# Hybrid decoder trunk on one core: the order of VectorE's softmax work in a head's step, and of the loads, tables and first products of the opening

## The chip, the cores and the metric

One core of a Trainium2 chip runs the whole program. The time is device time of that core in microseconds (us), from launch to end. The engines are TensorE (PE, its weight loads PEld), VectorE (DVE), ScalarE (ACT), GpSimd (POOL) and SyncE (SP, which issues most DMAs). Each has its own instruction stream, in the order in which the program is written; they meet at semaphores.

## What is computed

Two post-norm decoder layers over 256 tokens of 1024 features, float32. The part that matters here, cut from the reference:

```python
def hybrid_mixer(x, positions, w_in, ...):
    h = x @ w_in
    c_q, c_kv, k_rope, fox_qkv, fox_f, dil_qkv = jnp.split(h, cuts, axis=-1)
    q_a = to_heads(rms_norm(c_q, q_gain) @ w_uq, MLA_HEADS)        # 4 heads "MLA"
    kv_a = to_heads(rms_norm(c_kv, kv_gain) @ w_ukv, MLA_HEADS)
    ...
    o_b = causal_block_attention(q_b, k_b, v_b, cum_log_f)          # 6 heads "FOX"
    o_c = dilated_mixture_attention(rope(q_c, positions), rope(k_c, positions), v_c)   # 6 heads "DIL"
    return mixed @ w_out

for l in range(2):
    x = layer_norm(ALPHA * x + hybrid_mixer(x, ...), ...)
    x = layer_norm(ALPHA * x + memory_cross_attention(x, mem, ...), ...)
    gates = shared_group_router(x, router_w, router_bias)            # top-1 group, top-2 experts
    x = layer_norm(ALPHA * x + moe_ffn(x, gates, ...), ...)
```

Every softmax is over the keys of one query; a dilated head's exponentials are multiplied by how often a key falls into the three windows, and then summed.

## The kernel before

**Weights.** All weights come as a stream of pieces of up to 128x1024 float32, in the order of `weight_stream`: per layer A (4 pieces: the latents), FV, FK, FQ, UQ, UKV, DQ, DK, DV, MK, MV0, WO0, WO1 and so on, then the experts. SP loads a piece into a ring of 12 places (`raw`); a load waits until the piece 12 before it has been split. ACT copies a piece to its high part (`split_hi`, L562), DVE subtracts to get the low part (`split_lo`, L568); the two parts stand in a ring of 4 places (`w_split`), and a place is free when PE has used the piece (`split_free`). PE takes three products for each chunk, high*high, high*low, low*high (`product`, L1646 to L1648).

**The opening of layer 0.** x comes as two tiles of 128 tokens (XT0, XT1). PE turns each (`turn_x`, 8 transposes, L1737), ACT takes the high part (L759) and DVE the low part (L1119) into xT. PE then works through A (`gemm`, `rows`: each piece for token tile 0 and 1 in turn, banks 0 and 1), turns the memory tokens (`turn_memory`, L1635), and goes on with FV and FK. `warm(n)` (L1772) is n transposes of the identity whose result nobody reads. `constants` and `make_angles` are small DVE tables. POOL loads gains, forget bias and router bias with `small(0)` and one more DMA (L588 to L597), from its own queue (q0); SP's loads run in queue q1.

**Heads.** A loop over 20 steps `s` runs on PE, DVE and ACT; in a step each engine works on another of the 16 heads. PE's step: the products of the pieces `turns[l][s]` (one to three, mostly one), the values of heads s-5 and s-4 at odd s (`head_values`, L1865), the transposes of head s-3's probabilities (`head_turn`, L1844), the scores of head s-1 (`head_scores`, L1819 and L1820; for the DIL heads both of a pair at odd s, L1810), and the transposes of head s's q and k (`head_qk`). `head_turn` waits for the scaled probabilities of its head and for the copy of the head before it, since all use one PSUM bank (B_PT). DVE's step is in this order:

```python
                    for h in scored(s):
                        softmax_max(l, h)
                    if TURNED <= s < HEADS + TURNED:
                        evac_pT(l, s - TURNED)
                    if 2 <= s < HEADS + 2:
                        softmax_norm(l, s - 2)
                    for i in ahead_of[l][s]:
                        split_lo(dve, i)
                    if s >= VALUED and (s - VALUED) % 2 == 1:
                        ...
                        evac_o(l, s - VALUED)
```

`softmax_max` (L1142, L1145) writes scaled, masked scores to SBUF with their maximum, and then its negative; `softmax_norm` (L1161 for DIL heads, L1164, L1168) sums, inverts and scales the exponentials; `evac_pT` (L1178) copies transposed probabilities out of PSUM; `evac_o` (L1188) makes the low part of the heads' outputs (`mixT_lo`). ACT makes the exponentials (`exps`, L804) one step before `softmax_norm` takes them. `ahead_of[l][s]` are the pieces that PE uses two steps later. `rotate` (L658 to L664) is the rotary work on POOL.

**Before the experts.** The router's group choice `ing` (L1314) is DVE work; `gather` on PE waits for it. In layer 0 products of layer 1's memory keys stand ahead of that wait; in layer 1 `keep_busy(11)` does (L1767: 11 products of 128x512 that nobody reads).

## Time and profile before

| | us |
|---|---|
| median of 3 runs | 809.81 (809.38 to 812.72) |
| the profiled execution, its own time | 808.45 |
| span of its trace, first to last instruction | 806.8 |
| busy in it: PE / DVE / ACT / POOL | 785.0 / 629.0 / 506.8 / 77.4 |

The profiled execution is 1.36 us under the median of the three runs; 1.65 us of its time lie outside the span. Matmuls are pipelined and their ends are modelled, so a row of PE tells when it starts; how long a wait is, is best read from start to start. Engine rows that follow without a gap are merged with "x n".

### The profile page before, as it was taken

The page shows a single profiled execution, that of the slowest core. Times are in us where ns is not written, and L with a number is a line of the kernel's source. Part 1 is how long each engine was busy: PE and PEld are TensorE (multiplying, and loading weights), DVE is VectorE, ACT ScalarE, POOL GpSimd, SP SyncE. Part 2 cuts the span into 40 slices and gives each one's busy share as a digit, 9 for nine tenths or more (in the row PEclk, how much of TensorE's full clock was granted, in tenths as well). Part 3 has the DMA queues.
Part 4 walks back from the last instruction along what each step waited for, and adds up shares of the span by engine and source line. Part 5 has one row for each costly group of instructions (what it writes and reads, how often), then busy time and mean ns, then how long its engine had stood idle before and what let it go on. Part 6 is the DMA issues. An engine that isn't in the chain of part 4 may idle for free.

```text
span 806.8 us, 12012 instructions
## 1 busy us (share of the span) xinstructions
PE 785.0 (97%) x4311; PEld 677.0 (84%) x4311; DVE 629.0 (78%) x1110; ACT 506.8 (63%) x782; POOL 77.4 (10%) x150
## 2 busy tenths in 40 slices
PE   8999999999999999999999999989999999999995
PEld 7999996789888888888899988868998788888884
DVE  5657777785669999999874578887655799999995
ACT  4755564454547788888756566544443768888873
POOL 3159000020000000000011233002000000000000
PEclk9999999999999999999999999999999999999998
DMA  9964343575345799999956543426634349999951
GB/s 294 362 203 158 132 132 106 161 226 164 105 147 166 232 365 371 365 365 372 350 150 181 170 131 131 148 99 200 211 105 131 131 148 347 370 365 366 370 198 53
DMA packets 123117, 177.05 MB, mean 219 GB/s; under 512 B 10176, under 2 KB 92624, under 8 KB 123056
## 3 DMA queue, kind: packets, MB, share of 16 engines
q1 hardware_dynamic: 121072, 169.56, 62.9%
q0 software_dynamic: 1984, 6.70, 3.0%
q8 instruction: 36, 0.59, 0.3%
q14 instruction: 25, 0.20, 0.1%
HBM read 175.18 MB, written 1.05 MB: 218 GB/s over the span
## 4 chain that ended last, share of the span: by engine, by line
PE 86%; DVE 10%; issue 1%; DMA 1%; ACT 1%; DVEq 0%; SPq 0%; ACTq 0%
PE bank L1646 24%; PE bank L1648 23%; PE bank L1647 23%; DVE w_split L568 2%; PE bank L1831 2%; PE bank L1874 2%; PE bank L1844 2%; PE bank L1865 1%; DVE xg_lo L1582 1%; PE bank L1820 1%; PE bank L1984 1%; PE bank L1737 1%; PE bank L1800 1%; PE bank L1894 1%; DVE xs L1194 1%
## 5 line engine op out<-in xcount | busy, mean ns | idle before, releaser
L568 DVE TENSOR_TENSOR w_split<-raw,w_split 128x1024 fp32r<-128x1024 f32 (+3 forms) x334 | 383.7, 1172 | 68.6 <-ACT w_split L562 63.3
L562 ACT ACTIVATE w_split<-raw 128x1024 fp32r<-128x1024 f32 (+3 forms) x334 | 334.4, 1010 | 107.6 <-PE bank L1648 92.5
L1646 PE MATMUL bank<-w_split,xg_hi 128*128 128x512 f32 x256 | 102.9, 402 | 0.0
L1648 PE MATMUL bank<-w_split,xg_lo 128*128 128x512 f32 x256 | 100.1, 391 | 0.0
L1647 PE MATMUL bank<-w_split,xg_hi 128*128 128x512 f32 x256 | 99.9, 390 | 0.0
L1646 PE MATMUL bank<-w_split,xT_hi 128*128 128x384 f32 (+2 forms) x224 | 77.8, 347 | 0.1
L1648 PE MATMUL bank<-w_split,xT_lo 128*128 128x384 f32 (+2 forms) x224 | 75.8, 338 | 0.0
L1647 PE MATMUL bank<-w_split,xT_hi 128*128 128x384 f32 (+2 forms) x224 | 75.6, 338 | 0.0
L1648 PEld LDWEIGHTS bank<-w_split,xg_lo 128*128 128x128 f32 x256 | 48.0, 188 | 10.3
L1646 PEld LDWEIGHTS bank<-w_split,xg_hi 128*128 128x128 f32 x256 | 48.1, 188 | 9.4 <-DVE xg_lo L1582 0.5
L1647 PEld LDWEIGHTS bank<-w_split,xg_hi 128*128 128x128 f32 x256 | 48.2, 188 | 9.0
L1646 PE MATMUL bank<-w_split,mixT_hi 128*128 128x512 f32 x128 | 51.8, 404 | 2.0 <-DVE w_split L568 1.9
L1648 PE MATMUL bank<-w_split,mixT_lo 128*128 128x512 f32 x128 | 50.0, 391 | 0.0
L1647 PE MATMUL bank<-w_split,mixT_hi 128*128 128x512 f32 x128 | 50.0, 390 | 0.0
L1648 PE MATMUL bank<-w_split,aT_lo 128*128 128x512 f32 x128 | 49.8, 389 | 0.0
L1646 PE MATMUL bank<-w_split,aT_hi 128*128 128x512 f32 x128 | 49.8, 389 | 0.0
L1647 PE MATMUL bank<-w_split,aT_hi 128*128 128x512 f32 x128 | 49.8, 389 | 0.0
L1646 PEld LDWEIGHTS bank<-w_split,xT_hi 128*128 128x128 f32 x224 | 42.2, 188 | 1.1 <-DVE w_split L568 0.6
L790 ACT ACTIVATE qkT<-bank 66x512 f32<-66x512 f32 (+2 forms) x26 | 15.5, 595 | 42.9 <-PE bank L1800 29.5
L1647 PEld LDWEIGHTS bank<-w_split,xT_hi 128*128 128x128 f32 x224 | 42.3, 189 | 0.1
L1648 PEld LDWEIGHTS bank<-w_split,xT_lo 128*128 128x128 f32 x224 | 42.1, 188 | 0.0
L1178 DVE COPY probs<-bank 128x384 f32<-128x384 f32 (+1 forms) x40 | 23.3, 582 | 19.1 <-PE bank L1848 12.1
(325 smaller groups left out, 1531.4 us busy)
## 6 DMA issues: line engine op xcount, KB each, us to landing
raw<-in_expert_w_gate_dram SPq DMA_DIRECT2D x128, 256.0 KB, 5.9
raw<-in_expert_w_up_dram SPq DMA_DIRECT2D x128, 256.0 KB, 7.7
raw<-in_expert_w_down_dram SPq DMA_DIRECT2D x64, 512.0 KB, 7.7
raw<-in_xattn_w_kv_dram SPq DMA_DIRECT2D x32, 512.0 KB, 3.8
raw<-in_w_in_dram SPq DMA_DIRECT2D x40, 384.0 KB, 4.5
raw<-in_w_mix_out_dram SPq DMA_DIRECT2D x16, 512.0 KB, 3.4
raw<-in_xattn_w_q_dram SPq DMA_DIRECT2D x16, 512.0 KB, 3.4
raw<-in_xattn_w_o_dram SPq DMA_DIRECT2D x16, 512.0 KB, 5.3
```

Of the source, the lines that this page charges most:

```text
L562: nc.scalar.activation(halves_of(i)[0][:, 0:w], raw[:, i % RAW, 0:w], ACT.Copy).then_inc(hi_ready, 1)
L568: nc.vector.tensor_tensor(lo[:, 0:w], raw[:, i % RAW, 0:w], hi[:, 0:w].bitcast(F32), ALU.subtract).then_inc(lo_ready, 1)
L790: nc.scalar.activation(qkT[0:d, qk_slot(h), :], B_QK[0:d, :], ACT.Copy).then_inc(qkT_ready.sem, n)
L1178: nc.vector.tensor_copy(turned_of(h), B_PT[:, 0:w]).then_inc(pT_ready.sem, 1)
L1194: nc.vector.scalar_tensor_tensor(half, half, ALPHA, product, ALU.mult, ALU.add, accum_out=st[:, 2 * n_ + t, 2 * h:2 * h + 1]).then_inc(sig ...
L1582: nc.vector.tensor_tensor(xg_lo[:, f, :, :].rearrange("p g s -> p (g s)"), bank[XG_BANKS[f]][:, :], xg_hi[:, f, :, :].rearrange("p g s -> ...
L1646: nc.tensor.matmul(o, lhs[0], rhs[0], start=first, stop=False, skip_group_check=shared)
L1647: nc.tensor.matmul(o, lhs[0], rhs[1], start=False, stop=False, skip_group_check=shared)
L1648: return nc.tensor.matmul(o, lhs[1], rhs[0], start=False, stop=last, skip_group_check=shared)
L1831: ins = nc.tensor.matmul(o[:, t * T:(t + 1) * T], qTx[:, 2 * g + c_, t * P:(t + 1) * P], kTx[:, 2 * g + c_, :], start=c_ == 0, stop=c_ == 1)
L1844: ins = nc.tensor.transpose(B_PT[:, k * P:(k + 1) * P], pr[:, k * P:(k + 1) * P], ident[:, :])
L1874: ins = nc.tensor.matmul(value_bank(h)[:, dblk * T:(dblk + 1) * T], vx[:, c_, f * P:(f + 1) * P], turned_of(h)[:, c_ * T:(c_ + 1) * T], st ...
```

## The change

Four parts.

1. **DVE's step.** `softmax_norm(s-2)` moves to the front of the step, ahead of `softmax_max` and `evac_pT`. `softmax_max` of the 16 heads multiplies by minus the scale and takes the minimum, so that it writes the negated maximum itself, and its own negation (L1145) falls away; ACT's `exps` use scale -1, and wait for each token tile by itself. For the 6 DIL heads `evac_pT` moves to ACT, behind `evac_o` and ahead of the copies and `evac_qk`.
2. **The opening's products.** `warm(8)` is removed. XT0 and XT1 use banks 4 to 7 instead of 0 to 3. A's first three pieces are done for token tile 0 first and then for tile 1 (`by_tile`). ACT's and DVE's split of A's second piece stands ahead of XT1.
3. **The opening's loads and tables.** SP issues positions and memory tokens behind FV's four pieces instead of behind A's. POOL's four small loads wait until FV's second piece has landed, and stand behind its masks. DVE's and ACT's work on memory (`turn_memory`), angles and sines, and the A latents stand in another order; PE waits for the memory's low parts before UQ instead of before FK.
4. **Ahead of `gather` in layer 1** `keep_busy(11)` becomes `keep_busy(7)`.

The diff, cut:

```diff
@@ -304,6 +304,8 @@
...
         def pair_in(l, name, k):
+            if l == 0 and name in ("XT0", "XT1"):
+                return k + 2
             return 1 - k if l and k < 2 and job[name] >= job["MV0"] else k
@@ -534,7 +536,7 @@
...
                     tokens(1)
-                if i == index[0, "A", 3]:
+                if i == index[0, "FV", 3]:
                     sp.dma_start(pos_i[:, :], positions[0].rearrange("(t p) -> p t", p=P),
                                  allow_slow_non_contiguous=True).then_inc(pos_in, 16)
@@ -683,6 +683,10 @@
...
+            pool.wait_ge(raw_in[index[0, "FV", 1] % RAW], landed_value[index[0, "FV", 1]])
+            pool.nop().then_inc(paused_p, 1)
+            small(0)
+            pool.dma_start(rbias[:, :], router_bias.rearrange("(a n) -> a n", a=1).to_broadcast([P, NE])).then_inc(bias_in, 16)
             pool.wait_ge(mem_in, 16)
@@ -789,14 +793,21 @@
...
+            def evac_pT(l, h):
+                act.wait_ge(pt_done.sem, pt_done.at(l, h + 1))
+                act.wait_ge(o_done.sem, o_done.at(l, h - 1))
+                nc.scalar.activation(turned_of(h), B_PT[:, 0:3 * P], ACT.Copy).then_inc(pT_ready.sem, 1)
+
             def exps(l, h):
-                act.wait_ge(nmx_ready.sem, nmx_ready.at(l, h + 1))
+                if h >= HEADS:
+                    act.wait_ge(nmx_ready.sem, nmx_ready.at(l, h - HEADS + 1))
                 if h >= 3:
                     act.wait_ge(pt_done.sem, pt_done.at(l, free_turns(h)))
                 for t in range(TT):
                     if h < HEADS:
+                        act.wait_ge(s_masked.sem, s_masked.at(l, 2 * h + t + 1))
                         sl = slice(0, P) if t == 0 else slice(P, 3 * P)
-                        src, scale = probs_of(h)[:, sl], 1.0
+                        src, scale = probs_of(h)[:, sl], -1.0
@@ -882,14 +893,12 @@
                 turn_x(l, "XT0", 0)
                 if l:
                     turn_later(l)
+                    split_hi(act, first + 1)
                 else:
+                    split_hi(act, first + 1)
                     turn_x(l, "XT1", 1)
-                split_hi(act, first + 1)
                 for i in range(first + 2, first + 8):
                     split_hi(act, i)
-                if l == 0:
-                    turn_memory()
-                    sines()
@@ -927,6 +942,8 @@
                 for s in range(HEADS + VALUED):
                     if s >= VALUED and (s - VALUED) % 2 == 1:
                         evac_o(l, s - VALUED)
+                    if MLA_H + FOX_H + TURNED <= s < HEADS + TURNED:
+                        evac_pT(l, s - TURNED)
@@ -1139,10 +1155,8 @@
                     scale = float(MLA_D if h < MLA_H else HD) ** -0.5
                     for t in range(TT):
                         sl = slice(0, P) if t == 0 else slice(P, 3 * P)
-                        nc.vector.tensor_tensor_reduce(probs_of(h)[:, sl], score_bank(h)[:, sl], mask[:, P - P * t:2 * P], scale, -3e38,
-                                                       ALU.add, ALU.max, mx[:, h, t:t + 1]).then_inc(s_masked.sem, 1)
-                    dve.wait_ge(s_masked.sem, s_masked.at(l, 2 * h + 2))
-                    nc.vector.tensor_scalar(nmx[:, h, :], mx[:, h, :], -1.0, None, ALU.mult).then_inc(nmx_ready.sem, 1)
+                        nc.vector.tensor_tensor_reduce(probs_of(h)[:, sl], score_bank(h)[:, sl], mask[:, P - P * t:2 * P], -scale, 3e38,
+                                                       ALU.add, ALU.min, nmx[:, h, t:t + 1]).then_inc(s_masked.sem, 1)
@@ -1430,22 +1446,25 @@
...
+                    split_lo(dve, first + 1)
+                else:
                     split_lo(dve, first)
-                split_lo(dve, first + 1)
+                    turn_x(l, "XT0", 0)
+                    split_lo(dve, first + 1)
+                    turn_x(l, "XT1", 1)
                 split_lo(dve, first + 2)
                 split_lo(dve, first + 3)
                 if l == 0:
                     constants()
+                split_lo(dve, first + 4)
+                if l == 0:
                     make_angles()
-                for i in range(first + 4, first + 8):
+                for i in range(first + 5, first + 8):
                     split_lo(dve, i)
-                if l == 0:
-                    turn_memory()
@@ -1453,8 +1472,14 @@
...
-                for i in range(first + 8, first + 12):
-                    split_lo(dve, i)
+                split_lo(dve, first + 8)
+                split_lo(dve, first + 9)
+                if l == 0:
+                    turn_memory(range(2))
+                split_lo(dve, first + 10)
+                if l == 0:
+                    turn_memory(range(2, 4))
+                split_lo(dve, first + 11)
@@ -1494,12 +1519,12 @@
...
+                    if 2 <= s < HEADS + 2:
+                        softmax_norm(l, s - 2)
                     for h in scored(s):
                         softmax_max(l, h)
-                    if TURNED <= s < HEADS + TURNED:
+                    if TURNED <= s < MLA_H + FOX_H + TURNED:
                         evac_pT(l, s - TURNED)
-                    if 2 <= s < HEADS + 2:
-                        softmax_norm(l, s - 2)
                     for i in ahead_of[l][s]:
                         split_lo(dve, i)
@@ -1665,6 +1690,25 @@
...
+            def by_tile(l, js):
+
+                open_job(l, "A")
+                parts = {}
+                for t, b in enumerate(banks(l, "A")):
+                    last_half = evac_v[l][job[f"XT{t}"]]
+                    pe.wait_ge(job_v.sem, job_v.at(l, last_half - 1))
+                    for j in js:
+                        if t == 0:
+                            parts[j] = sub_in(index[l, "A", j])
+                        if j == 2:
+                            pe.wait_ge(job_v.sem, job_v.at(l, last_half))
+                        for k in range(2):
+                            lhs = tuple(v[:, 2 * j + k, t * P:(t + 1) * P] for v in xT)
+                            r = tuple(v[:, k * A_W:(k + 1) * A_W] for v in parts[j])
+                            ins = product(b[:, 0:A_W], lhs, r, j == 0 and k == 0, False)
+                        if t == TT - 1:
+                            ins.then_inc(split_free, 1)
@@ -1923,7 +1967,7 @@
...
                 else:
-                    keep_busy(11)
+                    keep_busy(7)
@@ -2049,21 +2093,22 @@
...
                     turn_x(l, "XT1", 1, 0)
-                    warm(8)
-                ready(l, "XT0")
-                pe.wait_ge(job_v.sem, job_v.at(l, evac_v[l][job["XT1"]] - 1))
-                for i in range(first + 0, first + 2):
-                    gemm(i)
-                ready(l, "XT1")
-                for i in range(first + 2, first + 4):
-                    gemm(i)
+                if l:
+                    ready(l, "XT0")
+                    pe.wait_ge(job_v.sem, job_v.at(l, evac_v[l][job["XT1"]] - 1))
+                    for i in range(first + 0, first + 2):
+                        gemm(i)
+                    ready(l, "XT1")
+                    gemm(first + 2)
+                else:
+                    by_tile(l, range(3))
+                gemm(first + 3)
                 if l == 0:
                     turn_memory()
                 for i in range(first + 4, first + 8):
                     gemm(i)
                 if l == 0:
                     pe.wait_ge(fp_tables, 3)
-                    pe.wait_ge(mem_v, 4)
```

What the change does to the order, at three places. First PE's opening of layer 0, before (bank7 with ident alone is `warm`):

```order
1 L1772 MATMUL bank7<-ident_57 128x128 x12
2 L1737 MATMUL bank0<-ident_57,xs_51 128x128 x4
4 L1737 MATMUL bank2<-ident_57,xs_51 128x128 x4
6 L1772 MATMUL bank7<-ident_57 128x128 x8
7 L1646 MATMUL bank0<-w_split_50,xT_hi_52 128x416
10 L1646 MATMUL bank1<-w_split_50,xT_hi_52 128x416
```

and the same place in the changed kernel:

```order
1 L1816 MATMUL bank7<-ident_57 128x128 x12
2 L1781 MATMUL bank4<-ident_57,xs_51 128x128 x4
4 L1781 MATMUL bank6<-ident_57,xs_51 128x128 x4
6 L1671 MATMUL bank0<-w_split_50,xT_hi_52 128x416
24 L1671 MATMUL bank1<-w_split_50,xT_hi_52 128x416
```

Eight transposes are gone, and 18 products of tile 0 (bank 0) now stand ahead of tile 1's first (bank 1), which were three.

Second, DVE at step 15 of layer 0, where the scores of heads 14 and 15 are taken, from the second of the two maxima, before (L1142 is `softmax_max`, L1178 `evac_pT`, L1161 to L1168 `softmax_norm` of head 13):

```order
206 L1142 ISA probs,mx<-bank,dilmask 128x256
207 L1142 ISA mx 128x1
208 L1145 TENSOR_SCALAR nmx<-mx 128x2
209 L1178 COPY probs<-bank 128x384
210 L1161 ISA probs,sm<-probs,dilcount 128x128
214 L1164 RECIPROCAL ri<-sm 128x2
215 L1168 TENSOR_SCALAR probs<-probs,ri 128x128
216 L1168 TENSOR_SCALAR probs<-probs,ri 128x256
217 L568 TENSOR_TENSOR w_split<-raw,w_split 128x1024
218 L1188 TENSOR_TENSOR mixT_lo<-bank,mixT_hi 128x256
```

and after, from the end of `softmax_norm` of head 13 (L1182):

```order
195 L1182 TENSOR_SCALAR probs<-probs,ri 128x256
196 L1158 ISA probs,nmx<-bank,dilmask 128x128
198 L1158 ISA probs,nmx<-bank,dilmask 128x256
200 L1158 ISA probs,nmx<-bank,dilmask 128x128
202 L1158 ISA probs,nmx<-bank,dilmask 128x256
204 L570 TENSOR_TENSOR w_split<-raw,w_split 128x1024
205 L1202 TENSOR_TENSOR mixT_lo<-bank,mixT_hi 128x256
```

The scaling has gone ahead of the maxima, the negation and the copy are gone, and the split of the next piece follows the second maximum directly.

Third, ACT in the same steps, before (L812 is `evac_o`, L804 `exps`):

```order
99 L812 ACTIVATE mixT_hi<-bank 128x256
100 L562 ACTIVATE w_split<-raw 128x1024
101 L804 ACTIVATE probs<-probs,nmx 128x128
102 L804 ACTIVATE probs<-probs,nmx 128x256
105 L562 ACTIVATE w_split<-raw 128x1024
```

and after (L799 is the copy `evac_pT`):

```order
105 L823 ACTIVATE mixT_hi<-bank 128x256
106 L799 ACTIVATE probs<-bank 128x384
107 L564 ACTIVATE w_split<-raw 128x1024
108 L815 ACTIVATE probs<-probs,nmx 128x128
112 L799 ACTIVATE probs<-bank 128x384
113 L564 ACTIVATE w_split<-raw 128x1024
```

Each step of the DIL heads has one copy more on ACT, ahead of the split.

## Rows read from the trace of the kernel before

**Rows 1.** The page: the chain that ended last, by engine.

```profile
PE 86%; DVE 10%; issue 1%; DMA 1%; ACT 1%; DVEq 0%; SPq 0%; ACTq 0%
```

**Rows 2.** PE's waits, 60 to 172 us (heads of layer 0): total, times, longest.

```profile
PE bank L1844 <- DVE probs L1168: 1.6, 2, 0.9
PE bank L1646 <- DVE w_split L568: 0.9, 2, 0.7
```

**Rows 3.** PE's waits, 457 to 565 us (heads of layer 1).

```profile
PE bank L1844 <- DVE probs L1168: 2.2, 3, 0.9
PE bank L1646 <- DVE w_split L568: 1.0, 2, 0.7
```

**Rows 4.** PE, 530 to 543 us: start, duration, work, [idle before it].

```profile
530.97 0.39 PE L1648 MATMUL bank<-w_split,mixT_lo 128*128 128x512 f32 x1
532.23 0.55 PE L1844 MATMUL bank<-ident,probs 128*128 128x128 f32 x3 [0.87 <-DVE probs L1168]
533.45 0.47 PE L1646 MATMUL bank<-w_split,mixT_hi 128*128 128x512 f32 x1 [0.68 <-DVE w_split L568]
...
541.47 0.87 PE L1865 MATMUL bank<-probs,dv 128*64 128x256 f32 x8 [0.65 <-DVE probs L1178]
```

**Rows 5.** DVE in order of time, 530 to 533 us.

```profile
530.27 0.56 DVE L1178 COPY probs<-bank 128x384 f32<-128x384 f32 x1
...
532.08 1.22 DVE L568 TENSOR_TENSOR w_split<-raw,w_split 128x1024 fp32r<-128x1024 f32 x1
```

**Rows 6.** DVE in order of time, 468 to 474 us.

```profile
468.50 0.55 DVE L1168 TENSOR_SCALAR probs<-probs,ri 128x128 f32<-128x128 f32 x2
...
471.07 0.29 DVE L1142 CUSTOM_DVE_ANT_0 probs<-bank,causal 128x128 f32<-128x128 f32 x1 [0.91 <-PE bank L1820]
...
472.49 1.50 DVE L1168 TENSOR_SCALAR probs<-probs,ri 128x128 f32<-128x128 f32 x2
```

**Rows 7.** PE in order of time, 9 to 21 us.

```profile
9.61 1.91 PE L1772 MATMUL bank<-ident 128*128 128x128 f32 x8
11.38 0.58 PE L1646 MATMUL bank<-w_split,xT_hi 128*128 128x416 f32 x1
...
11.99 0.35 PE L1648 MATMUL bank<-w_split,xT_lo 128*128 128x416 f32 x1
12.18 0.35 PE L1646 MATMUL bank<-w_split,xT_hi 128*128 128x416 f32 x1
...
20.64 1.91 PE L1635 MATMUL bank<-ident,mem_tok 128*128 128x128 f32 x16
```

**Rows 8.** ACT, then DVE, in order of time, 7 to 20 us.

```profile
18.40 0.86 ACT L562 ACTIVATE w_split<-raw 128x780 fp32r<-128x780 f32 x1 [0.20 <-DMA raw<-in_w_in_dram]
19.45 0.86 ACT L562 ACTIVATE w_split<-raw 128x780 fp32r<-128x780 f32 x1 [0.20 <-DMA raw<-in_w_in_dram]
...
7.66 1.28 DVE L1119 TENSOR_TENSOR xT_lo<-bank,xT_hi 128x512 fp32r<-128x512 f32 x2
10.48 1.29 DVE L1119 TENSOR_TENSOR xT_lo<-bank,xT_hi 128x512 fp32r<-128x512 f32 x2 [1.54 <-ACT xT_hi L759]
```

**Rows 9.** Queue q0, 6 to 11 us; A's second piece; POOL's wait for memory.

```profile
q0 software_dynamic: 143, 0.21, 40.6%
...
L503 SPq DMA_DIRECT2D raw<-in_w_in_dram x1: 433/433/433, 2.3 to 2.3; - x1
...
DMA to landing us min/median/max: 8.3/8.3/8.3
...
16.85 0.56 POOL L672 DMA_DIRECT2D gb<-in_ln_mix_g_dram  x1 [9.72 <-DMA mem_tok<-in_mem_dram]
```

**Rows 10.** Layer 1 ahead of gather: PE, DVE, and busy time with granted clock.

```profile
639.29 4.36 PE L1767 MATMUL bank<-memT_hi,ones 128*128 128x512 f32 x11
...
642.36 0.17 DVE L1314 TENSOR_TENSOR ing<-rt 128x8 fp32r<-128x8 f32 x1
...
640.00:642.00 2.00, 2.00 (x6) 1.54 (x5) 1.73 (x11) 1.97 (x3) 0.00 (x0) 0.50 0.66 254
```

30 lines of the change are left out of this document (18 added, 12 removed).

## The prediction

> **What bounds the kernel now.** I read the chain that ended last first: PE has 86% of it and DVE 10% [rows 1]. So the end moves only where PE waits, or where it does work that nobody needs. There are three such places. PE's waits in the heads of layer 0 are 1.6 us for scaled probabilities and 0.9 us for a split [rows 2]; in layer 1 they are 2.2 and 1.0 us [rows 3], and one of 0.65 us for a copy [rows 4]. Next the opening: from 9.61 us PE does eight dummy transposes, and A's products begin at 11.38 us [rows 7]. Last, ahead of gather in layer 1, eleven dummy products begin at 639.29 us and take about 4.2 us, though `ing`, for which PE waits behind them, is made at 642.36 us (0.17 us long) [rows 10].
>
> In order of time the waits in the heads show what is late. PE starts the last product of a piece at 530.97, and the transposes of head 13 only at 532.23: 1.26 us where these products follow each other every 0.23 us, so 1.03 us are lost, of which the row calls 0.87 idle [rows 4]. DVE was meanwhile at the copy of 530.27, then at head 13's scaling, and turned to the split of the next piece at 532.08, which takes 1.22 us; that split ends at 533.3, and PE's next piece starts at 533.45 [rows 4, 5]. The exponentials of head 13 are a step old by then: the scaling is late only because it stands behind work that waits for PE's newest scores.
>
> **The heads.** The added order costs nothing by itself: same instructions, less one negation (about 0.17 us, by the small DVE instruction of L1314 [rows 10]) in each of 32 steps. With the scaling first, `head_turn` need not wait: in layer 1 head 13's scaling starts as soon as DVE is free, before the scores. Behind the scores DVE then has two maxima and, with the copy gone to ACT, goes directly to the split. At 530.27 the maxima were over; without two negations they end near 530.1, but the scaling of about 1.3 us, now ahead of them, partly pushes them to about 530.5. The split then ends near 531.7 instead of 533.3, and PE gains 1.0 us on the transposes and 0.65 us on the next piece, 1.65 us here. The same pair of waits stands in layer 0. Idle times of 2.5 us in layer 0 and 3.85 us in layer 1 are 6.3 us over ten waits [rows 2 to 4]; from start to start the example loses 0.16 us more (1.03 against 0.87) [rows 4]; on some eight of them that is 1.3 us, so at most 7.6 us. What stays: the wait at 541.47, head 15's values, is 0.65 us, and it is the way from transposes to copy to values; ACT's copy of such a tile is hardly shorter than DVE's 0.56 us, so I leave 0.5 us of it [rows 4, 5]. That gives **7.1 us**. The lower bound is nothing, if each wait goes over to another releaser; the upper 7.6.
>
> What hides the moved work: DVE idles 0.91 us before a maximum [rows 6], and a clean scaling is 0.55 us for its two tiles [rows 6]. Beside POOL's rotary work the same two instructions took 1.50 us [rows 6]; there the front of the step overflows by about 0.8 us (0.15 of reciprocal with it), and maximum, exponentials and copy come that much later. PE asks for that copy only behind the next piece's 12 products, 2.1 us at least (an estimate for 128x384, from 0.19 us for 128x416 [rows 7]), so I cost it at nothing; without this cover it would be 0.8 us in some four steps a layer. The six copies on ACT stand ahead of `evac_qk` and the splits; ACT is busy for 506.8 of 806.8 us and has them at the same PE event for which it waits in that step anyway, so nothing.
>
> At this place a rule of the Trainium skill bears. SBUF — State Buffer, section "SBUF: two separate sides", says that DVE in a two-port mode and GpSimd share one port pair as an exclusive lock, held for a whole instruction. The trace agrees (0.55 against 1.50 us [rows 6]). By it, what matters is under which POOL work the scaling falls, not how long it is; it speaks against putting it ahead of the maxima, and by it the sum would be some 6 us smaller at worst (0.8 us, four steps, two layers), which I take up as a rival from the rows.
>
> **The opening.** Without the eight transposes A's first products could start at 9.61 [rows 7]. They need tile 0's low part, from 7.66 on two instructions of 1.28 us together, so 8.9 [rows 8]; in the order of before they would also need tile 1's first half, half of the 1.29 us from 10.48, so 11.1 [rows 8]: `by_tile` is what makes the 1.8 us usable. But the eight dummies started every 0.22 us (1.77 us from 9.61 to 11.38), half the pace of the sixteen of the memory, which take 1.91 us; the products of 128x416 follow every 0.19 us from 11.99 on [rows 7]. So until about 11.7 PE is at the lower of its two clock levels (1.2 against 2.4 GHz), and the first six products take about 2.1 us instead of 1.1. After them comes A's second piece: it landed at 10.6 (2.3 + 8.3) [rows 9], while POOL's small loads held 40.6% of the DMA engines from 6 to 11 us, 2.0 us of them [rows 9]. With these loads later I take 8.6, and its low part at 10.5: no wait. The third piece lands near 10.5, is split behind tile 1 on both engines, and is there at 12.9, some 0.05 to 0.1 us late. Then 42 more products at 0.19 us: A ends near 19.65 instead of 20.64 [rows 7]. **1.0 us.** Bounds: if the second piece still lands at 10.6, everything behind it is 1.9 us later, and A ends about 0.9 us later than before; at best (no slow clock) it ends 1.8 us earlier.
>
> The memory tokens come next. They had landed by 16.85 [rows 9]; behind FV's four pieces they land where FV's fourth did. Its second was taken at 18.40 and its third at 19.45, both just as they landed, so one piece is 1.05 us of queue and the fourth landed at 20.5, the latest that I allow [rows 8]; but as the small loads' 2.0 us are issued only after FV's second piece has landed, most of them fall behind the memory: 18 to 18.5. PE asks at 19.65: no wait, and 0.85 us at the upper bound. The rest of part 3 (latents, angles, sines, memory parts) I cost at nothing: PE reads none of it before FK's end, 18 us later.
>
> The Trainium skill, TensorE: Matmul & The Clock Gate, section "Part 4: PE-mode transpose", says that transposes do not count as PE-busy for the clock. By the trace the products kept the full pace 0.6 us after the first had started, behind 36 transposes and nothing else (28 of them before 9.61) [rows 7], so here they count. By the page the eight dummies did nothing, and their removal would leave the products alone to raise the clock: about 1 us more of slow products, and the opening would gain nothing.
>
> **Gather.** The granted clock from 640 to 642 us was 0.50 [rows 10], so each dummy took about 0.4 us. Seven end near 641.9, `ing` is there at 642.5, and PE goes on at 642.5 instead of 643.5: 1.0 us in an execution with this low clock. At full clock eleven take about 2.5 us and end before `ing`: nothing. And if the idle 0.6 us keep the clock low, PE's eight products of 128x512 behind it take 1.8 us longer. I take **0.5 us** (bounds -0.8 and 1.0).
>
> **Sum.** 7.1 + 1.0 + 0.5 = 8.6 us. Against the profiled execution (808.45) that is 799.85; it was 1.36 us under the median of the runs, and the median is the measure: 809.81 - 8.6 = **801.2 us**. Behind these places PE's chain has no clock of its own to wait for, so I expect nothing to be given back.
>
> **The rivals.**
> - *The waits change their releaser.* Behind the turned wait stands the split (0.68 of its own at 533.45) and the low part of the outputs; one that stays late keeps half of the heads' gain: 7.1 to 3.5, 804.8 us. For it: DVE's next work is already behind. Against: it was late only by the scaling and the copy. Chance 0.15.
> - *The opening gives nothing*: the second piece lands late, or the clock stays low as the page's rule would have it, or PE waits for memory; 1.0 becomes 0 to -0.9, so 802.2 to 803.1 us. Chance 0.12.
> - *Slower than before.* The scaling at the front waits for ACT's exponentials of the step before, and holds the maximum behind it. Place: every step of both layers; price: what exponentials end later than the scores, plus the scaling (0.7 us clean, 1.65 beside POOL) less DVE's 0.91 us of idle. It decides against the change from 0.27 us lost on PE in each of 32 head steps, 8.6 us; at 0.4 us the time is 814. Against: exponentials were done before the scores in the steps of which rows show waits, and PE has a piece of 2.1 us between. With the POOL steps alone, up to 6 us are lost, 807. Chance 0.07 (0.04 of it above 813).
> - *More than I count*: shorter steps also take away small delays before the transposes of q and k; 798. Chance 0.06.
>
> My forecast, 799 to 803.5 us, has 0.60. The range 798.5 to 805.5 leaves out the slow rival and the ends of the first and the last. A measurement tells about 0.5%, 4 us, from no change. Faster by over that (under 805.8): 0.60 + 0.12 + 0.06 + 0.08 of the first rival = 0.86; within: 0.10; slower: 0.04.
>
> **What would show it.** Right: no wait of the head transposes (L1844 before) on the scaling in either layer; 1 us or less of PE waits left in each; A's first product near 9.6, with five slow ones behind it; memory transposes near 19.7; POOL's small loads at 13 to 16 us. Wrong: `softmax_norm` preceded by long idle on ACT's exponentials, or by PE waits on qkT or the maxima; A's second piece split after 11 us; PE waiting for mem_tok; a granted clock of 0.5 behind gather or in the opening past 12 us.

## The result, and where the time went

The changed kernel takes **803.91 us** in the median of four runs (803.51 to 804.43), against 809.92 us (809.38 to 812.72) of the kernel before in the same session: ratio 0.9915, 95% interval 0.9891 to 0.9938, so it is between 5.0 and 8.8 us faster. Forecast were 801.2 us and a saving of 8.6; the measured time lies 0.4 us above the 799 to 803.5 us that were held most likely, and inside the range of 798.5 to 805.5. The profiled execution took 803.51 us with a span of 801.9 us, where that of before had 806.8. In the chain that ended last PE's share has grown from 86% to 88%, and DVE's has fallen from 10% to 8% [rows 1]:

```profile
PE 88%; DVE 8%; issue 1%; ACT 1%; DMA 1%; DVEq 0%; SPq 0%; ACTq 0%
```

PE's waits, by what it waited for (us in total, times, longest): from 60 to 172 us there is none left [rows 2]. From 457 to 565 us, in the heads of layer 1 [rows 3], all waits for scaled probabilities are gone, and of the others one, for a split, has grown to 1.4 us:

```profile
PE bank L1671 <- DVE w_split L570: 1.4, 1, 1.4
PE bank L1909 <- ACT probs L799: 0.6, 1, 0.6
```

The surest reading of such a pair of traces is to take the PE instruction at the same place in the order in both and to subtract its starts. The difference is the time saved up to there; it is flat over hundreds of instructions and steps only where something happened. Inside A, where the order of the products differs, it compares equal counts of products: the 13th is the first of A's second piece before, and the first of its third piece after.

| PE instruction | start before | start after | saved |
|---|---|---|---|
| A's 13th product | 13.88 | 13.06 | 0.82 |
| first transpose of the memory tokens (end of A) | 20.64 | 19.91 | 0.73 |
| transposes behind the first wait of layer 0's heads | 74.11 | 72.47 | 1.64 |
| first output piece behind layer 0's heads | 144.53 | 140.46 | 4.07 |
| a product of layer 1's memory keys, behind layer 0's router | 250.65 | 247.66 | 2.99 |
| piece behind head 13's transposes, layer 1 | 533.45 | 526.14 | 7.31 |
| piece behind head 15's values, layer 1 | 542.69 | 536.40 | 6.29 |
| first dummy product ahead of gather, layer 1 | 639.29 | 634.90 | 4.39 |
| first product for `ing` | 643.49 | 638.19 | 5.30 |
| last product of PE | 797.04 | 791.87 | 5.17 |

So the opening gave 0.7 to 0.8 us, and the heads by these rows 3.25 and 4.3 us less 1.0. Counted over the heads alone (from the starts of 59.98 and 457.00 us of before) they gave 3.3 and 4.5 us less 1.0, 6.7 in all; the rest is small differences between the two. Ahead of the `ing` products there are two places at which time was **lost** that was already saved: 1.1 us in layer 0 and 1.9 us in layer 1. Both stand under half clock. Busy time in stretches of 2 us (PE, PEld, DVE, ACT, POOL, granted clock, DMA share, GB/s) of the changed kernel, layer 0 and then layer 1:

```profile
242.00:244.00 2.00, 2.00 (x21) 2.00 (x20) 1.74 (x3) 1.13 (x2) 0.49 (x1) 1.00 0.47 193
244.00:246.00 2.00, 2.00 (x16) 2.00 (x16) 1.73 (x9) 1.82 (x3) 0.00 (x0) 0.80 1.05 272
246.00:248.00 2.00, 2.00 (x11) 2.00 (x11) 1.07 (x8) 0.84 (x2) 0.00 (x0) 0.50 0.86 281
...
628.00:630.00 2.00, 0.76 (x5) 0.53 (x6) 1.74 (x4) 1.69 (x4) 0.00 (x0) 1.00 0.04 15
630.00:632.00 2.00, 2.00 (x15) 2.00 (x15) 1.79 (x3) 1.94 (x3) 1.04 (x2) 0.72 0.10 18
632.00:634.00 2.00, 2.00 (x11) 2.00 (x11) 1.23 (x1) 0.12 (x1) 0.00 (x0) 0.50 0.99 356
634.00:636.00 2.00, 2.00 (x8) 1.81 (x9) 0.59 (x3) 0.91 (x2) 0.00 (x0) 0.50 0.95 293
```

In the trace of the kernel before, the only half clock between the opening and the end began at 639.77 us, under the dummies [rows 10]. There it cost at most what the dummies ran past the making of `ing`, about 1 us. Now it begins at 630.89 us, under the router's products, on which everything waits. The rows of PE show the same by pace: the first router group takes 0.60 us for four products, those behind it 1.0 us. Gather's products follow right behind the seven dummies:

```profile
630.30 0.60 PE L2211 MATMUL bank<-w_split,xT_hi 128*128 128x32 f32 x4
630.75 0.89 PE L2216 MATMUL bank<-w_split,xT_lo 128*128 128x16 f32 x4
631.49 1.01 PE L2211 MATMUL bank<-w_split,xT_hi 128*128 128x32 f32 x4
...
634.90 3.15 PE L1811 MATMUL bank<-memT_hi,ones 128*128 128x512 f32 x7
638.19 0.27 PE L1974 MATMUL bank<-ing,upto 128*128 128x4 f32 x1
```

The new wait at the end of layer 1's heads is read from ACT and DVE, in order of time. ACT stands idle for 2.61 us until PE's transposes of head 15 are done, copies them, and only then makes the two splits that are queued behind; DVE's half of the first split, for which PE waits 1.43 us, starts at 535.03:

```profile
530.46 0.49 ACT L799 ACTIVATE probs<-bank 128x384 f32<-128x384 f32 x1
533.57 0.49 ACT L799 ACTIVATE probs<-bank 128x384 f32<-128x384 f32 x1 [2.61 <-PE bank L1888]
533.95 1.99 ACT L564 ACTIVATE w_split<-raw 128x1024 fp32r<-128x1024 f32 x2
```

```profile
536.40 0.47 PE L1671 MATMUL bank<-w_split,mixT_hi 128*128 128x512 f32 x1 [1.43 <-DVE w_split L570]
```

Before, the copy was DVE's, and ACT made the same two splits directly behind the head outputs.

The opening, PE in order of time. The eight transposes of tile 1 take 1.09 us, and the products behind them run at 0.19 us from the start, so PE was at its upper clock level; the granted clock reads full from 6.25 us on. In place of slow products there are two waits, for the low parts of A's second and third piece:

```profile
7.88 1.09 PE L1781 MATMUL bank<-ident,xs 128*128 128x128 f32 x8 [1.32 <-DMA xs<-in_x_dram]
8.73 0.43 PE L1671 MATMUL bank<-w_split,xT_hi 128*128 128x416 f32 x1
9.00 0.35 PE L1672 MATMUL bank<-w_split,xT_hi 128*128 128x416 f32 x1
...
10.93 0.46 PE L1671 MATMUL bank<-w_split,xT_hi 128*128 128x416 f32 x1 [0.82 <-DVE w_split L570]
...
13.06 0.46 PE L1671 MATMUL bank<-w_split,xT_hi 128*128 128x416 f32 x1 [0.73 <-DVE w_split L570]
...
19.91 1.25 PE L1660 MATMUL bank<-ident,mem_tok 128*128 128x128 f32 x10
```

### The profile page after: what moved, and what is told of

It reads as the page before. It is cut to its first block, busy times and chain, and to the rows that moved or that the text cites. A ratio compares the mean times of both kernels' runs of the same rounds, so it can differ in the third digit from the quotient of the medians.

```text
span 801.9 us, 11957 instructions
## 1 busy us (share of the span) xinstructions
PE 782.4 (98%) x4299; PEld 677.3 (84%) x4299; DVE 620.0 (77%) x1066; ACT 511.7 (64%) x794; POOL 79.3 (10%) x150
## 4 chain that ended last, share of the span: by engine, by line
PE 88%; DVE 8%; issue 1%; ACT 1%; DMA 1%; DVEq 0%; SPq 0%; ACTq 0%
PE bank L1671 24%; PE bank L1673 24%; PE bank L1672 24%; DVE w_split L570 2%; PE bank L1875 2%; PE bank L1918 2%; PE bank L1888 2%; PE bank L1909 1%; DVE xg_lo L1607 1%; PE bank L1844 1%; PE bank L1864 1%; PE bank L1938 1%; DVE xs L1208 1%; DMA raw<-in_w_in_dram 1%; PE bank L1781 1%
## 5 line engine op out<-in xcount | busy, mean ns | idle before, releaser
L1671 PE MATMUL bank<-xT_hi,w_split 128*128 128x256 f32 x112 | 32.4, 289 | 0.0
```

The costliest lines, as they stand in the source:

```text
L1671: nc.tensor.matmul(o, lhs[0], rhs[0], start=first, stop=False, skip_group_check=shared)
```

## The experiments

Twelve further runs were made, one of them the changed kernel again. The theory for all: each part removes what the start-to-start table shows, independently of the others, and the rest of the difference to the forecast is half clock. The rivals: the parts shift waits to each other; or ACT's copies, not the place of the scaling, make the heads' gain. "Saved" is always by PE's starts against the kernel before; for the heads it is counted over the heads alone, as above.

### The heads alone, and the opening alone

Heads alone is the kernel before with only `softmax_norm`, `softmax_max`, `exps` and `evac_pT` of the diff; opening alone is the rest of it, with eleven dummies.

> The kernel before with the heads' part alone (scaling at the front, negated scores, six copies on ACT). In the trace of the changed kernel PE's starts in the heads of layer 0 come 3.25 us earlier than before, in layer 1 4.32 us earlier and then 1.03 us of it are lost again. If the parts are independent, this kernel gains the sum, 6.5 us of 809.9: 803.4 us, with no PE wait over 0.3 us in the heads of layer 0, and with waits of about 0.6 and 1.4 us at the end of the heads of layer 1. Stretches of half clock may move the time by 1 to 3 us either way, and the saving from start to start between them should stay 6.5. Rival (the opening shifts DVE's and POOL's work under the heads and gives part of it): under 5 us from start to start.

> The kernel before with the opening's parts alone (no dummies, products by tile, loads and tables moved; 11 dummies ahead of gather, heads as before). A ends 0.8 us earlier, nothing else moves: 809.1 us, PE's waits in the heads 2.5 and 3.9 us as before. In the changed kernel's trace the clock was full from 6.25 us on, before only from 11.71; if the full clock again comes at 6.25 the waits for the second and third piece (0.8 us each) stand, and if it comes late the first products are slow instead and A ends about as much earlier (0.5 to 0.9 us). Rival (the whole 0.8 us was the earlier clock): with full clock from 11 us on nothing is saved at the end of A.

Heads alone: 803.86 us (803.05 to 805.87), ratio 0.9918 (0.9895 to 0.9941). The heads save 3.3 us in layer 0 and 4.5 less 1.0 in layer 1, the same steps as in the whole change, at the same instructions: 6.7 us. The rival, that the opening feeds the heads' gain, falls. Opening alone: 809.0 us, ratio 0.9979 (0.9961 to 0.9996): 1.7 us faster, with 0.3 to 3.2 inside the interval.

The opening of before, in the trace of the heads' run, showed a wait of PE that had not been there:

```profile
19.47 1.91 PE L1642 MATMUL bank<-ident,mem_tok 128*128 128x128 f32 x16
32.05 0.41 PE L1653 MATMUL bank<-w_split,xT_hi 128*128 128x384 f32 x1 [2.12 <-DVE w_split L568]
```

In that execution PE was 1.2 us ahead of [rows 7] at the memory transposes, without any change of the opening: the granted clock rose at 5.42 us instead of 11.71. It lost this and more at FK. DVE makes FK's low parts behind the latents (29.65 us; 28.49 before), which wait for ACT's squares, and these stood behind memory copies and a table load. About half of the wait has another source: FV's fourth piece landed later in this execution, and ACT took it at 22.04 us instead of 20.90, behind 1.45 us of waiting for it:

```profile
22.04 0.85 ACT L562 ACTIVATE w_split<-raw 128x780 fp32r<-128x780 f32 x1 [1.45 <-DMA raw<-in_w_in_dram]
```

None of the twelve traces with the new order has a wait at FK: the latents come at 24.3 to 27.4 us there. So the order of latents, memory and sines, which I had priced at nothing, seems to be what lets PE keep a gain made further ahead. No run moves this order by itself, so its own share is not shown.

The opening alone also showed what its two new waits can bring, by the granted clock:

```profile
12.00:14.00 2.00, 1.27 (x5) 1.23 (x5) 2.00 (x5) 0.04 (x1) 0.58 (x1) 0.71 1.08 387
14.00:16.00 2.00, 2.00 (x8) 1.92 (x7) 0.38 (x4) 0.00 (x0) 1.76 (x4) 0.50 1.04 383
```

The saving stood at 1.14 us at A's 13th product and at -0.55 behind this stretch: 1.7 us lost.

### The small loads back at their old place

```diff
+            small(0)
+            pool.dma_start(rbias[:, :], router_bias.rearrange("(a n) -> a n", a=1).to_broadcast([P, NE])).then_inc(bias_in, 16)
             nc.gpsimd.memset(causal[:, :], 0.0).then_inc(const_pool, 1)
...
             pool.wait_ge(raw_in[index[0, "FV", 1] % RAW], landed_value[index[0, "FV", 1]])
             pool.nop().then_inc(paused_p, 1)
-            small(0)
-            pool.dma_start(rbias[:, :], router_bias.rearrange("(a n) -> a n", a=1).to_broadcast([P, NE])).then_inc(bias_in, 16)
```

> The changed kernel with POOL's small loads and the router's bias at their old place, at POOL's start. If they delay A's second piece: its low part is ready at 12 to 12.5 us instead of 10.88, PE's wait ahead of the second piece is 2 us or more instead of 0.85, and A ends 1 us or more later, after the kernel before: 804.9 us. Rival (the second piece is bound by ACT and DVE, which split it): PE's wait stays at 0.8 us, and A ends at the same time.

805.65 us (804.08 to 808.01), ratio 0.9937 (0.9898 to 0.9976). ACT in order of time: the second piece is taken 2.56 us later than in the changed kernel (8.91):

```profile
11.47 0.90 ACT L564 ACTIVATE w_split<-raw 128x832 fp32r<-128x832 f32 x1 [3.60 <-DMA raw<-in_w_in_dram]
```

The saving at A's 13th product is -1.74 us instead of +0.82. So the opening's gain hangs on the moved loads; with the products by tile and without the dummies, but with the loads at their old place, the opening ends 1.8 us later than before. The expected low part at 12 to 12.5 us started at 12.40; PE's wait ahead of it is 1.15 us, less than the 2 expected, since here the clock rose late and the first products were slow.

### The heads' two halves: copies back on DVE, scaling back at the end

```diff
-                    if MLA_H + FOX_H + TURNED <= s < HEADS + TURNED:
-                        evac_pT(l, s - TURNED)
...
-                    if TURNED <= s < MLA_H + FOX_H + TURNED:
+                    if TURNED <= s < HEADS + TURNED:
                         evac_pT(l, s - TURNED)
```

> The changed kernel with the six copies of transposed probabilities back on DVE, between the maxima and the split; the scaling stays at the front and the scores negated. If the scaling's place alone removes PE's waits for scaled probabilities and the copies those for the split: from start to start the heads of layer 0 save 1.9 us instead of 3.25 (0.8 and 1.0 at the transposes, nothing at the splits) and those of layer 1 2.7 us instead of 4.3, but the loss of 1.03 us at their end is gone, since no copy stands before ACT's splits: 4.6 instead of 6.55 in all, some 805.5 us. Rival (the scaling does it all, DVE had slack for the copy): 3.25 and 4.3 with no loss at the end, 7.5 in all, 802.8 us.

```diff
-                    if 2 <= s < HEADS + 2:
-                        softmax_norm(l, s - 2)
                     for h in scored(s):
                         softmax_max(l, h)
                     if TURNED <= s < MLA_H + FOX_H + TURNED:
                         evac_pT(l, s - TURNED)
+                    if 2 <= s < HEADS + 2:
+                        softmax_norm(l, s - 2)
```

> The changed kernel with the scaling of DVE's step back at its old place behind the maxima (and behind the copies of the other heads); negated scores and ACT's copies stay. DVE then has 0.17 us of negation and 0.55 us of copy less ahead of the scaling, so of each wait of about 1 us for scaled probabilities 0.7 us go: if it is so, the heads of layer 0 save 2.5 to 3 us and those of layer 1 3.5 to 4, and the place of the scaling was worth 1 us or less. Rival (the place is what counts): the five waits for scaled probabilities stand at 0.5 us or more each and the heads save under 4 us together.

Copies on DVE: 803.09 us (802.54 to 805.06), ratio 0.9923 (0.9906 to 0.9940), saved 2.7 us in layer 0 and 4.1 in layer 1 with nothing lost at its end, 6.8 together, as much as with ACT's copies (6.7). PE's waits in its layer 1:

```profile
PE bank L1907 <- DVE probs L1190: 0.6, 1, 0.6
PE bank L1669 <- DVE w_split L570: 0.4, 1, 0.4
```

Scaling at the end: 809.76 us, ratio 0.9998 (0.9983 to 1.0013), saved 1.4 us in layer 0 and nothing in layer 1 (1.0 won, 1.0 lost at its end). PE's waits in its layer 1:

```profile
PE bank L1671 <- DVE w_split L570: 2.1, 2, 1.4
PE bank L1888 <- DVE probs L1182: 1.4, 2, 0.7
PE bank L1909 <- ACT probs L799: 0.6, 1, 0.6
```

I had expected the opposite division (most of the gain without the place of the scaling), and that fell. With ACT's copies and the negated scores in both, the place is worth 5.3 of the 6.7 us. Two of the three waits for scaled probabilities in layer 1 stayed, behind the products of 470.87 and 488.01 us, 0.97 and 1.09 us from start to start as before. They are those of heads 1 and 5, whose copies are DVE's in both kernels; the third, head 13's, whose copy is now ACT's, is gone. Nor did the missing negation help these two. At head 5 DVE comes to the scaling sooner behind its maxima, but its two instructions then take 1.78 us instead of 1.49, and they end 0.15 us behind the end of POOL's rotary instruction of 487.89 us:

```profile
486.60 0.55 DVE L1192 COPY probs<-bank 128x384 f32<-128x384 f32 x1
487.26 1.78 DVE L1182 TENSOR_SCALAR probs<-probs,ri 128x128 f32<-128x128 f32 x2
```

```profile
487.89 1.00 POOL L660 TENSOR_TENSOR rot<-dk,sinb 128x384 f32<-128x384 f32 x1
```

The negation by itself was not run: no kernel here has the scaling at the front and the scores not negated. By DVE's rows its removal shortens the maxima of one head from 0.76 to 0.56 us and those of a pair from 1.63 to 1.12; what share of the 5.3 us needs it is not shown.

### Splits ahead of the last copy

```diff
+                    held = l and s == HEADS + TURNED - 1
-                    if MLA_H + FOX_H + TURNED <= s < HEADS + TURNED:
+                    if MLA_H + FOX_H + TURNED <= s < HEADS + TURNED and not held:
                         evac_pT(l, s - TURNED)
...
                     for i in ahead_of[l][s]:
                         split_hi(act, i)
+                    if held:
+                        evac_pT(l, s - TURNED)
```

> The changed kernel with one reordering on ACT in layer 1: the two splits of the last head steps stand ahead of the copy of head 15's transposed probabilities instead of behind it. If that copy, which waits for PE's transposes, is what made the splits late (ACT idle 2.61 us before it, then the split at 533.95, DVE's half at 535.03, PE's wait of 1.43 us), the wait is gone and the end of the heads comes 1.0 to 1.4 us earlier: 802.7 us. Rival (the splits wait for their piece or their slot anyway): the same splits at the same time and no gain, and the copy late by up to 2 us, 804 to 806 us.

By the trace the theory holds. ACT makes the two splits first and does the copy behind them, and PE's wait for the split is gone, the one for the copied probabilities (0.58 us) stays:

```profile
531.82 0.49 ACT L799 ACTIVATE probs<-bank 128x384 f32<-128x384 f32 x1
532.21 2.00 ACT L564 ACTIVATE w_split<-raw 128x1024 fp32r<-128x1024 f32 x2
534.93 0.49 ACT L799 ACTIVATE probs<-bank 128x384 f32<-128x384 f32 x1 [0.71 <-PE bank L1891]
```

The saving goes from 5.95 to 6.42 us there instead of from 7.31 to 6.29: 1.5 us. The time does not show it: 805.15 us (803.28 to 806.05), ratio 0.9928 (0.9905 to 0.9952). In the profiled execution there was half clock from 12.9 to 16.3, 245.0 to 248.4 and 630.7 to 644.4 us, in which 1.6, 1.2 and 3.5 us of saved starts went again. By the time alone it would have been read as a loss.

### Dummies ahead of gather, and in the idle stretch ahead of the router

```diff
-                    keep_busy(7)
+                    keep_busy(11)
```

> The changed kernel with 11 dummy products again instead of 7 ahead of gather in layer 1. If the stretch there is at half clock: four dummies of 0.42 us more, 1.3 to 1.7 us behind the making of ing, so 804.8 to 805.5 us. If it is at full clock: eleven take 2.5 us, ing is made 3.2 us after the last score product, no difference. Rival (dummies are what brings the full clock back): with 11 the full clock returns earlier and the time is equal or under that of 7.

```diff
-                    keep_busy(6)
+                    keep_busy(12)
```

> The changed kernel with twelve dummy products instead of six in layer 1 while PE waits for the second half of the normalized tokens: PE's idle stretch of 1.41 us there is filled (six at 0.23 us). If that idle stretch is what brings the clock down behind it (half clock from 630.89 to 637.71), there is no half clock between 626 and 645, the router's products save 1.9 us, and the seven dummies ahead of gather end early and cost nothing: 2 to 3 us less than the changed kernel's 803.9, or 801.5 us. Rival (the router's narrow products of 16 and 32 columns are what it answers to, or it comes by chance of where it falls): half clock stands again somewhere between 630 and 645 and the time is that of the changed kernel.

Eleven: 802.17 us (801.86 to 804.34), ratio 0.9895 (0.9873 to 0.9916). I had expected it to be slower than the changed kernel under half clock, and it was not. Twelve ahead of the transposes, with seven behind: 803.14 us (800.73 to 803.36), ratio 0.9909 (0.9892 to 0.9925). PE is fed there and the clock holds until 633.8 us, through all the router's products, so the 1.9 us that the changed kernel lost there are kept (the repeat below, which is not fed, kept them too, so this does not show the feeding). But the clock falls under the dummies. The seven, four of them still at full clock, end early, PE idles for `ing`, and gather runs at half clock behind it:

```profile
632.81 2.49 PE L1811 MATMUL bank<-memT_hi,ones 128*128 128x512 f32 x7
636.09 0.37 PE L1974 MATMUL bank<-ing,upto 128*128 128x4 f32 x1 [0.79 <-DVE ing L1330]
```

```profile
634.00:636.00 2.00, 1.30 (x4) 0.49 (x2) 1.69 (x12) 1.97 (x4) 0.00 (x0) 0.50 0.92 258
636.00:638.00 2.00, 1.91 (x7) 1.81 (x8) 1.40 (x6) 2.00 (x3) 0.00 (x0) 0.50 0.29 102
638.00:640.00 2.00, 2.00 (x6) 1.52 (x6) 2.00 (x3) 0.52 (x1) 0.00 (x0) 0.50 0.04 8
```

Over all traces the two numbers of dummies differ by about 1 us in the mean. Saved from the end of layer 1's heads (the product that starts at 542.69 us before) to PE's end; where half clock lay within 535 to 545 us of a kernel's own time, from behind it:

| kernels with | saved, each trace | mean |
|---|---|---|
| seven dummies | -1.1, -3.5, -0.8, -1.1, -0.8, -0.7, -0.9 | -1.3 |
| eleven dummies | 0.0, 0.0, -1.6, -0.1, -0.1, +0.3 | -0.2 |

Gather ran at half clock in five of the seven traces with seven dummies; with eleven, in one of six and there for its first 0.8 us. (In the row of seven, one trace, and in the row of eleven, two have the twelve ahead of the transposes as well.) In four of these traces (both of -1.1, the -3.5 and the -1.6) half clock began under the router's products, well ahead of the dummies, so not all of the difference is gather's. Where it began within 1.2 us of the dummies' start, it lasted 3.4 us in each of the five traces with eleven and in that of before, and 6.8 us in each of the four with seven. So the early end of the seven did not bring half clock on; the half clock was there already, and stayed longer.

### The changed kernel again, and three steps on top of each other

The repeat; then splits first with eleven dummies; then with twelve ahead of the transposes as well; and then, in the opening:

```diff
                         if t == 0:
+                            if j:
+                                for _ in range(5):
+                                    nc.tensor.transpose(bank[2][:, 0:P], ident[:, :], ident[:, :])
                             parts[j] = sub_in(index[l, "A", j])
```

> The changed kernel itself again, as the bar for the other three of this call: PE's starts save 0.8 us in the opening, 3.3 in the heads of layer 0 and 3.3 in those of layer 1, as in its first trace. If the stretches of half clock are a matter of where they fall in an execution, at least one of them (245.18 to 248.59 and 630.89 to 637.71 in the first trace) begins at another place or is missing; if they follow from the order of the work, both stand at the same places within 1 us. 803.9 us either way.

> The changed kernel with the two splits ahead of the last copy in layer 1, and eleven dummies ahead of gather again. The splits save 1.5 us at the end of the heads of layer 1, as in the trace of the run that moved them alone. Seven dummies that end early leave PE idle for about 1.2 us ahead of gather and gather then ran at half clock in three traces; if the eleven avoid that, 1 to 2 us more: 801.0 us. Rival (the half clock comes with eleven as well, as in the trace of the run with eleven alone, and the dummies only cost): 803 us or the time of the repeat.

> The run with the splits moved and eleven dummies, and twelve dummies instead of six ahead of the second half's transposes in layer 1. With PE fed at both places the only stretch with little activity is that of the router's narrow products: if the idle stretches bring the half clock, there is none between 626 and 650 us and it takes 2 us less than the run with the splits and eleven dummies, 799.5 us. Rival (the narrow products are enough, as in layer 0, where no idle stands ahead of the half clock at 245 us): half clock stands there still, and it is 0 to 1 us faster.

> The run before with five dummy transposes ahead of each of PE's two waits for A's second and third piece (0.85 and 0.8 us idle in the changed kernel's trace). In two of six traces with these waits the clock fell at 12.9 us, for 1.65 us lost. If the idle brings that, the stretch is gone, and with full clock at 6 us the transposes (0.11 us each) cost nothing: 0.5 us less in the median. Rival (where the clock comes late, at 11.4 to 11.7 us, the transposes take 0.21 us each and stand in PE's way): up to 1 us slower than the run before.

| kernel | median, us | range | ratio to before |
|---|---|---|---|
| changed kernel again | 802.97 | 800.12 to 805.74 | 0.9903 (0.9877 to 0.9930) |
| splits first, eleven dummies | 801.84 | 799.56 to 802.75 | 0.9885 (0.9862 to 0.9908) |
| and twelve ahead of the transposes | 801.03 | 798.64 to 801.94 | 0.9878 (0.9855 to 0.9900) |
| and the opening fed | 800.91 | 799.96 to 805.15 | 0.9895 (0.9869 to 0.9922) |

The repeat shows that the place of half clock does not follow from the order of the work. The order is the same, and layer 0 had full clock where the first trace had 0.80 and 0.50 (same columns as above):

```profile
244.00:246.00 2.00, 2.00 (x20) 2.00 (x19) 1.74 (x10) 1.98 (x2) 0.00 (x0) 1.00 1.01 217
246.00:248.00 2.00, 1.76 (x13) 1.27 (x11) 1.40 (x7) 1.72 (x4) 0.00 (x0) 1.00 0.83 270
```

Its half clock lay at 535.34 to 538.75 and 634.33 to 641.15 us instead. Its opening saved 1.1 to 1.3 us, and its heads 3.3 and 4.5 less 1.0, as in the first trace. With PE fed at both places ahead of gather (third row) only the router's narrow products are left, and half clock began at 631.28 us all the same, 0.5 us ahead of the dummies. It lay mostly under them, but so it did in the second row, without the feeding (632.97 us), and from the end of the heads to PE's end the two lose the same, 0.07 and 0.06 us. So the feeding has shown nothing, and my expectation of it fell; what has shown something are the eleven dummies. The fourth step can't be told from the third by the times; in its trace the clock rose late and the transposes stood in PE's way: 0.18 us saved at A's 13th product, where the run with DVE's copies, whose clock rose as late, had 0.84.

The second and the third row are 1.1 and 1.9 us under the changed kernel in the median. The intervals overlap; by starts, the splits' 1.5 us are in each of the four traces that have them. And there is more at that place. In three of the seven traces with the wait of 1.4 us there, half clock began within 0.7 us behind it (at 535.3, 535.8 and 541.1 us) and cost another 1.6 us; in none of the seven traces without it did half clock begin there.

## Why the forecast came out as it did, step by step

- **The heads, 7.1 us**: 6.7 measured. Right in mechanism and place. The waits for scaled probabilities went completely, in each of the eleven traces with the new place; what stays is the wait for head 15's copied probabilities, 0.58 us where I left 0.5. Layer 0 gave 3.3, more than its 2.5 us of idle, as the allowance for start-to-start had it.
- **"ACT ... has them at the same PE event for which it waits in that step anyway, so nothing."** This step failed. At the last head of layer 1 ACT waits for nothing else in that step, and two splits stand behind the copy. The price was 1.5 us, by the run that turned the two around. The rival that waits change their releaser came true here, in one place.
- **The split of the gain** inside the heads I had not priced. The copies on ACT are worth nothing beside the scaling's place (6.7 us with them, 6.8 without): they win 0.9 us (3.3 against 2.7 in layer 0, 4.5 against 4.1 in layer 1) and lose 1.0 at that end.
- **The lock between DVE and POOL** (the Trainium skill, SBUF — State Buffer, section "SBUF: two separate sides"): in layer 0 DVE was busy with the 32 scaling instructions for 13.0 us instead of 10.8, in layer 1 for 11.1 instead of 10.9. I read the 2.2 us as waiting for POOL's instructions; the trace agrees with the rule. As costed, PE's piece covered it.
- **The opening, 1.0 us**: at A's end 0.73 in the profiled execution, 1.14 in the repeat. The second piece's low part I put at 10.5 us and it was 10.88, the third at 12.9 and it was 13.01. The slow first products did not come in that execution; waits of 0.82 and 0.73 us stood in their place. In the run with the copies on DVE the clock did rise late (the eight transposes of tile 1 took 1.97 us, the first product came at 9.44 us, five slow ones stood behind it), and the third piece started at 13.04 us, the same: whichever comes, its split binds. That nearly as much was saved by another course of events than the one forecast is partly luck. The loads came as forecast: POOL's small ones from 13.78 us on, the memory tokens there by 18.50. The Trainium skill's rule on transposes (TensorE: Matmul & The Clock Gate, section "Part 4: PE-mode transpose") is again not what is seen: the transposes at 7.88 us follow each other at 0.11 us and nothing but transposes had run.
- **Gather, 0.5 us**: the sign was wrong. In the profiled execution the seven dummies save 0.9 us, as costed; over seven traces against six they cost about 1 us. The bound of -0.8, "if the idle 0.6 us keep the clock low", was the likelier end: behind the idle stretch 1.6 to 1.75 us of saved starts went in four traces, and 2.4 in a fifth.
- **"Behind these places PE's chain has no clock of its own to wait for, so I expect nothing to be given back."** This is the step that cost most: 1.1 and 1.9 us were given back to half clock in the profiled execution, 3.0 of the 8.3 that its places had won by the rows of the start-to-start table (0.8, 6.55 and 0.9). The kernel before had none of it at a place that costs in the one execution that I had, and I took that for a property of the kernel. In its 17 runs beside the first experiments it took 808.64 to 814.36 us. The mean granted clock of these runs was 0.992 to 0.994 in the five fastest and 0.987 to 0.988 in the three slowest, so half clock is at least part of this scatter; the times alone don't show it. That the forecast held in spite of 3.0 us that it had at nothing is in part luck: the other terms were nearly whole in that execution, and the range was wide enough for the rest.

## What to carry to other kernels

Put the work whose inputs are oldest first in an engine's in-order step, ahead of what waits for the newest result: that was 5 us here, with the negation gone as well. When a copy is handed to another engine, look at what is queued behind it there in every step, the last above all. Account for a change by the starts of the same instructions in two traces, and look at the granted clock at every step of that difference before calling it a cause.

## What was not expected of the hardware

Where PE's half clock falls is not set by the program alone. It lay over layer 0 between 243.8 and 251.8 us in seven of fourteen traces, whatever their edits, and in one of two of the same kernel; each stretch there cost 1.1 to 1.2 us. In layer 1 one began between 630.7 and 640.9 us in all fourteen. In layer 0 PE was never idle for 0.1 us in the 8 us ahead of it: what runs there are transposes and the router's narrow products. In the opening full clock came between 5.2 and 6.7 us in nine traces and between 11.2 and 11.8 in five, with the same first instructions. The Trainium skill, TensorE: Matmul & The Clock Gate, section "What's actually happening", says that the chip's looks at PE's activity run freely and do not reset when a kernel starts. The traces are in keeping with this, with one kernel meeting half clock at 245.2 and 630.9 us in one execution and at 535.3 and 634.3 in another. What decides between the two for a given stretch stays open: no run here measures it by itself. And the clock column reads 1.00 ahead of the first change that the trace records: from 8 to 12 us it read 1.00 in the run with DVE's copies, while products of 128x416 started every 0.35 us from 9.93 to 11.31. There the pace of the starts tells the clock, not the column.
